# Stage transitions by token tile in a two-block transformer on one core: transposes of the second tile moved among products of the first, and half of the modulations moved to VectorE

## The chip, the cores and the metric

One core of one Trainium2 chip runs the whole program in one launch. The metric is device time in microseconds (us), the median of the timed runs. A lower number is better.

## The reference, cut to what matters

`x` has 256 tokens and 1024 features in fp32. Two blocks follow each other, each of depth 2:

```
# first block; sh, sc, g come from silu(c) @ ada_w + ada_b
h = rms_norm(x, norm_mix[i]) * (1 + sc1) + sh1
y = chunked_relpos_attention(h)  if i == 0 else  chunked_spatial_gating(h)
x = x + g1 * y
h = rms_norm(x, norm_ffn[i]) * (1 + sc2) + sh2
x = x + g2 * (square(relu(h @ w1)) @ w2)          # 1024 -> 4096 -> 1024
# second block
h = rms_norm(x, pre_norm_g[l]);  proj = h @ w_in[l]
y = concat(diff_attention, gqa_attention) @ w_out[l]
x = x + rms_norm(y, post_norm_g[l])
```

So the residual stream `x` goes six times through the same kind of joint: a matmul stage ends, `x` is updated, each token's sum of squares gives a scale, the scaled `x` is transposed and modulated, and the next matmul stage begins. The first joint (the start of the program) and the end are not changed. The five in the middle are called T1 (attention to first mlp), T2 (first mlp to the gate values of spatial gating), T3 (spatial gating to second mlp), T4 (second mlp to the first layer of the second block) and T5 (that layer to the next).

## The kernel before, in words

**Precision.** Every fp32 operand is kept as two parts of type fp32r, a high part and a low part (value minus high part), and a product is three matmuls (`matmul3`, L1596 to L1598): high by high, high by low, low by high.

**Weights.** They stream from memory in chunks of 128 x 2048 through a buffer `raw` of four half chunks (`load`, L357, on the SP queue, which waits until the half four places earlier has been turned into its low part). ScalarE copies a half to `w_hi` (`hi_part`, L534), VectorE subtracts it from raw to get `w_lo` (`lo_part`, L949). `w_hi` and `w_lo` hold four chunks. A chunk is split by both engines in their own written order, and TensorE waits for the low part (`chunk_in`).

**Adaptive rows.** The sums for sh, sc and g (48 + 48 "ada" chunks of 1 MB) are made by VectorE (`ada`, eight instructions at L972 and L976 and a sum at L980), spread over the stages. `columns` (L1663) lets TensorE sum them over partitions, 32 matmuls of one column for a whole set, and `modulation` (three small VectorE instructions) turns them into scale and shift.

**The joint.** VectorE makes the residual (`residual`: product with the gate L1060, sum L1053, per token tile of 128 and half of the columns), ScalarE the sum of squares (`squares`, L551), GpSimd the inverse root (L437, L440), VectorE the scaled tokens `xn` (`norm_x`, L1020). TensorE issues `keep_warm` products with a zero row (L1681, 14 or 16 of them), then `transpose_x`: the 8 transposes of tile 0, then the 8 of tile 1 (L1645), into four banks that each hold both tiles of two feature blocks. ScalarE modulates the pairs of blocks (L560, in the second block L806), VectorE splits them into `h_hi` (L1027) and `h_lo` (L1030) in `operand`. The next stage's first product needs the first pair with both token tiles.

**The mlp stage** (`mlp_stage`) has 8 groups of 512 hidden features: two `up` products with weights as the stationary operand (48 matmuls of 256 columns each, so the result has features on partitions), relu and square on ScalarE (L713, L715) and VectorE (L1278, L1282, `mlp_half`), and two `down` products (24 matmuls of 512 columns each) that accumulate into four banks which were set to zero first (`zero_banks`, L1883). In the first mlp VectorE also makes two ada sums in each group. All engines go through their lists in written order; a wait stops everything behind it on that engine.

## Time and profile before

| | |
|---|---|
| timed runs | 1123.58, 1637.33 and 1128.87 us, median 1128.87 |
| the profiled execution's own time | 1119.04 us |
| its span | 1117.4 us |
| mean granted TensorE clock | 0.957 of full speed |
| TensorE busy (matmuls) | 1073.6 us, 96% |
| VectorE busy | 766.9 us, 69% |
| ScalarE busy | 554.4 us, 50% |

The span runs from the first to the last instruction of one execution. Busy TensorE time counts every matmul, also the products with a zero row, so 96% does not say that 96% of the time goes into products that the result needs. Times in the rows are microseconds from the start of the span.

### The profile page before, as it was taken

What the parts mean: (1) busy time and instruction counts of PE and PEld (TensorE: products, weight loads), DVE (VectorE), ACT (ScalarE), POOL (GpSimd) and SP (SyncE); (2) the same over time, 40 slices, a digit from 0 to 9 for tenths busy, and PEclk for the clock granted to TensorE, in tenths of its full rate; (3) what the DMA queues carried; (4) which work ended last, traced back from release to release, by engine and by line L of the source; (5) the groups of instructions that cost most, each with busy time, mean ns of one, the idle gap of its engine ahead of it and who ended that gap; (6) DMA issues with size and microseconds to landing.
All of it is one profiled execution on the core that took longest, in us unless ns stands there. A gap on an engine that the chain in (4) does not pass through costs nothing.

```text
span 1117.4 us, 18346 instructions
## 1 busy us (share of the span) xinstructions
PE 1073.6 (96%) x6096; PEld 923.0 (83%) x6096; DVE 766.9 (69%) x1352; ACT 554.4 (50%) x933; POOL 94.1 (8%) x146
## 2 busy tenths in 40 slices
PE   6999999999999999999999999999999989799897
PEld 6887776999899788889998789998878768688775
DVE  5798766988876667777877554565487564686573
ACT  1556775354434457444443443454365572556562
POOL 0121101000000100100000000000011020120100
PEclk9799997999999899999999899999999989899999
DMA  9866654778786458765765365456166410457211
GB/s 369 322 242 222 213 191 170 267 279 281 269 297 241 165 191 292 254 231 206 260 224 180 99 214 195 151 190 215 47 220 225 131 57 20 136 200 215 79 33 52
DMA packets 58071, 219.12 MB, mean 196 GB/s; under 512 B 6532, under 2 KB 12420, under 8 KB 51880
## 3 DMA queue, kind: packets, MB, share of 16 engines
q1 hardware_dynamic: 49232, 170.02, 44.5%
q0 software_dynamic: 5760, 41.95, 10.4%
q10 hardware_dynamic: 3032, 6.57, 1.8%
q8 instruction: 24, 0.39, 0.1%
q14 instruction: 23, 0.19, 0.1%
HBM read 217.46 MB, written 1.06 MB: 196 GB/s over the span
## 4 chain that ended last, share of the span: by engine, by line
PE 80%; issue 8%; DVE 4%; DMA 3%; ACT 3%; POOL 1%; DVEq 0%; ACTq 0%; SPq 0%; POOLq 0%
PE ps L1596 24%; PE ps L1597 23%; PE ps L1598 23%; PE ps L1691 2%; DMA ada_raw<-in_adastream 2%; PE ps L1663 2%; PE ps L1681 1%; PE ps L1645 1%; ACT ada_raw L631 1%; DVE w_lo L949 1%; PE ps L1655 1%; POOL rinv L440 1%; PE ps L1958 1%; PE ps L2064 1%; DMA arena<-in_adastream 1%
## 5 line engine op out<-in xcount | busy, mean ns | idle before, releaser
L949 DVE TENSOR_TENSOR w_lo<-raw,w_hi 128x1024 fp32r<-128x1024 f32 (+1 forms) x318 | 358.8, 1171 | 62.0 <-ACT w_hi L534 56.0
L534 ACT ACTIVATE w_hi<-raw 128x1024 fp32r<-128x1024 f32 (+1 forms) x318 | 308.4, 1008 | 129.8 <-DMA raw<-in_wstream 94.2
L1596 PE MATMUL ps<-h_hi,w_hi 128*128 128x256 f32 x704 | 202.3, 287 | 0.5 <-DVE h_lo L1030 0.3
L1597 PE MATMUL ps<-h_lo,w_hi 128*128 128x256 f32 x704 | 200.7, 285 | 0.0
L1598 PE MATMUL ps<-h_hi,w_lo 128*128 128x256 f32 x704 | 200.7, 285 | 0.0
L1596 PE MATMUL ps<-w_hi,h_hi 128*128 128x512 f32 (+1 forms) x480 | 192.7, 401 | 3.2 <-DVE h_lo L1030 3.2
L1597 PE MATMUL ps<-w_lo,h_hi 128*128 128x512 f32 (+1 forms) x480 | 187.3, 390 | 0.0
L1598 PE MATMUL ps<-w_hi,h_lo 128*128 128x512 f32 (+1 forms) x480 | 187.0, 390 | 0.0
L1596 PEld LDWEIGHTS ps<-h_hi,w_hi 128*128 128x128 f32 x704 | 136.6, 194 | 3.5 <-issue 2.0
L1596 PE MATMUL ps<-w_hi,a_hi 128*128 128x512 f32 x352 | 137.4, 390 | 0.7 <-DVE a_lo L1359 0.7
L1597 PEld LDWEIGHTS ps<-h_lo,w_hi 128*128 128x128 f32 x704 | 136.7, 194 | 0.7
L1597 PE MATMUL ps<-w_lo,a_hi 128*128 128x512 f32 x352 | 137.2, 390 | 0.0
L1598 PE MATMUL ps<-w_hi,a_lo 128*128 128x512 f32 x352 | 137.0, 389 | 0.0
L1598 PEld LDWEIGHTS ps<-h_hi,w_lo 128*128 128x128 f32 x704 | 136.5, 194 | 0.0
L1596 PEld LDWEIGHTS ps<-w_hi,h_hi 128*128 128x128 f32 x480 | 92.3, 192 | 24.4 <-DVE h_lo L1030 2.8
L1598 PEld LDWEIGHTS ps<-w_hi,h_lo 128*128 128x128 f32 x480 | 92.4, 193 | 19.0
L1597 PEld LDWEIGHTS ps<-w_lo,h_hi 128*128 128x128 f32 x480 | 92.5, 193 | 16.5
L713 ACT ACTIVATE arena<-ps 128x512 f32<-128x512 f32 x32 | 19.1, 598 | 148.8 <-PE ps L1598 148.8
L1278 DVE TENSOR_TENSOR arena<-arena 128x512 f32<-128x512 f32 x32 | 22.1, 689 | 88.7 <-ACT arena L713 88.7
L1596 PEld LDWEIGHTS ps<-w_hi,a_hi 128*128 128x128 f32 x352 | 66.2, 188 | 14.4 <-issue 1.2
L1598 PEld LDWEIGHTS ps<-w_hi,a_lo 128*128 128x128 f32 x352 | 66.1, 188 | 13.7
L1597 PEld LDWEIGHTS ps<-w_lo,a_hi 128*128 128x128 f32 x352 | 66.2, 188 | 12.9
(186 smaller groups left out, 1341.9 us busy)
## 6 DMA issues: line engine op xcount, KB each, us to landing
raw<-in_wstream SPq DMA_DIRECT2D x296, 512.0 KB, 5.3
ada_raw<-in_adastream POOLq DMA_DIRECT2D x40, 1024.0 KB, 5.1
ada_raw<-in_adastream SPq DMA_DIRECT2D x4, 1024.0 KB, 9.2
arena<-in_adastream SPq DMA_DIRECT2D x4, 1024.0 KB, 10.7
raw<-in_wsmall SPq DMA_DIRECT2D x22, 128.0 KB, 2.2
row<-in_gate_rows ACTq DMA_DIRECT2D x5, 512.0 KB, 4.3
row<-in_params ACTq DMA_DIRECT2D x2, 769.0 KB, 4.1
x<-in_x SPq DMA_DIRECT2D x1, 1024.0 KB, 9.4
```

The source lines that it names most:

```text
L440: nc.gpsimd.tensor_tensor(dst, mean, half[:, 0:cols_n], ALU.pow).then_inc(done, 1)
L534: act.activation(w_hi[:, c % SPLIT, at], raw[:, n, 0:width // 2], ACT.Copy)\
L631: last = act.activation(v, v, ACT.Copy, scale=cond[:, k:k + 1])
L713: act.activation(relu[:, u, :], ps[:, 4 + u, :], ACT.Relu).then_inc(s_upread, 1)
L949: nc.vector.tensor_tensor(w_lo[:, c % SPLIT, at], raw[:, (2 * c + h) % RAW, 0:width // 2], w_hi[:, c % SPLIT, at].bitcast(F32), ALU.subtract)\
L1278: own.inc(nc.vector.tensor_tensor(squared[:, u, :], relu[:, u, :], relu[:, u, :], ALU.mult))
L1596: nc.tensor.matmul(dst, sh, mh, start=start, stop=False)
L1597: nc.tensor.matmul(dst, sh, ml, start=False, stop=False)
L1598: return nc.tensor.matmul(dst, sl, mh, start=False, stop=stop)
L1645: last = nc.tensor.transpose(ps[:, 4 + pr, b * S + t * P:b * S + (t + 1) * P], xn[:, t, k * P:(k + 1) * P], ident[:])
L1663: last = nc.tensor.matmul(ps[:, bank, b:b + 1], ada_acc[:, a, (b % 2) * P:(b % 2 + 1) * P], ones[:, 0:1], start=True, stop=True)
L1691: last = nc.tensor.matmul(ps[:, 0, 2 * a + b:2 * a + b + 1], first_ada[a][:, k, b * P:(b + 1) * P], cond[:, k:k + 1], start=k == 0, stop=k ...
```

## The change

All five joints go tile by tile. (a) The last `down` products of a stage finish token tile 0 before tile 1 begins (`last_downs`), where before only the last of the two hidden parts was ordered by tile; the spatial gating stage now ends so too, with `columns` between the tiles, and without its four closing zero products; in T1 `columns` moves in front of tile 1's last two steps. (b) VectorE's list takes tile 0's residual, tile 1's first half, `norm_x` of tile 0, tile 1's second half, then the operands by tile and by half of the features. (c) TensorE issues 4 zero-row products, transposes tile 0, issues 8 more, and starts products of tile 0; tile 1 is transposed between the first and the second half of those. (d) Features 0 to 3 of each tile (of 8 blocks) are modulated by VectorE, 4 to 7 by ScalarE, in instructions of 128 x 128 instead of 128 x 256. (e) The first group of each mlp is made tile by tile with tokens as the stationary operand. Its result lies with tokens on partitions, so ScalarE copies it out of the bank (`upraw`), TensorE transposes it (`turn_up`, 4 transposes for each half), and only then come relu and square. In this group both `ada` sums stand behind both `mlp_half`, and the second mlp gets two such sums (46 and 47) that the gating stage made before. (f) The second block's joint key and value weights come as one chunk instead of four small ones. (g) The loops over the two halves of the gating stage and over the two layers of the second block are written out.

```diff
-WARM = (14, 16, 16, 16)
+WARM = (4, 8)
...
+            def mlp_first(c0, m0):                              # ScalarE
+                for u in range(2):
+                    act.wait_ge(s_used, c0 + u + 1)
+                    act.activation(squared[:, u, :], ps[:, 2 * u, :], ACT.Copy)\
+                        .then_inc(s_upraw, 1)
+                    act.wait_ge(s_upT, m0 // 14 + u + 1)
+                    act.activation(relu[:, u, :], ps[:, 4 + u, :], ACT.Relu).then_inc(s_upread, 1)
+                    act.wait_ge(s_upread, 2 + m0 + u + 1)
+                    act.activation(a_hi[:, u].rearrange("p a b -> p (a b)"), relu[:, u, :],
+                                   ACT.Square).then_inc(s_acthi, 1)
+                for j in range(4):
+                    split(c0 + 3 + j)
...
+            def operands(n, before_second, behind):             # VectorE
+                operand(0, 0, n)
+                norm_x(1, n)
+                operand(0, 1, n)
+                before_second()
+                operand(1, 0, n)
+                operand(1, 1, n)
+                behind()
+
+            def transition(ready, n, at_first, before_second, behind):
+                residual(0, 0, ready)
+                residual(0, 1, ready)
+                at_first()
+                residual(1, 0, ready)
+                norm_x(0, n)
+                residual(1, 1, ready)
+                operands(n, before_second, behind)
...
+                mlp_half(m0, lambda v: v)                       # first group of an mlp, VectorE
+                split(c0 + 3)
+                mlp_half(m0 + 1, lambda v: v)
+                for a in ((20, 21) if with_ada else (46, 47)):
+                    ada(a)
+                for c in (c0 + 4, c0 + 5, c0 + 6):
+                    split(c)
...
-            keep_warm(7, WARM[0])
-            transpose_x(1)
-            mlp_stage(0, 0, 8, 20, 24)
...
+            def transition(count):                              # TensorE
+                keep_warm(7, WARM[0])
+                transpose_x(0, count)
+                keep_warm(7, WARM[1])
...
+            def last_downs(c, m, between=None):
+                for t in range(TT):
+                    for u in range(2):
+                        if t == 0:
+                            chunk_in(c + 2 + u)
+                            pe.wait_ge(s_act, m + u + 1)
+                        for cb in range(2):
+                            last = down_products(c, u, t, cb, u == 1)
...
+                    if t == 0 and between is not None:
+                        between()
+
+            def mlp_stage(layer, m0, n, a_gate, a_cols):
+                c0 = C_FFN[layer]
+                transition(2 * n)
+                chunk_in(c0)
+                up_tile(c0, 0, 0, range(4), 4 * n + 4)
+                transpose_x(1, 2 * n)
+                up_tile(c0, 0, 0, range(4, KT), 4 * n + 4)
+                chunk_in(c0 + 1)
+                up_tile(c0, 1, 0, range(KT), 4 * n + 4)
+                up_tile(c0, 0, 1, range(KT), 4 * n + 4)
+                up_tile(c0, 1, 1, range(4), 4 * n + 4)
+                turn_up(0, 2 * layer)
+                up_tile(c0, 1, 1, range(4, KT), 4 * n + 4)
+                for bank in (0, 1, 3):
+                    zero_bank(bank)
+                turn_up(1, 2 * layer)
+                zero_bank(2)
+                for u in range(2):
+                    down(c0, u, m0 + u, None, 4, lambda v: v)
+                with pe.Fori(0, 6) as i:
...
-            out_step(2, 0, 1)                                   # T1, TensorE
+            out_step(2, 1, 0)
             pe.wait_ge(s_norm, 16)
             transpose_out(3)
-            out_step(2, 1, 0)
-            out_step(2, 1, 1)
+            out_step(2, 0, 1)
             pe.wait_ge(s_pTc, 16)
             pe.wait_ge(s_ada, 12)
             gate_sum(8, (6, 7))
-            for t in range(TT):
-                for cb in range(2):
-                    out_step(3, cb, t)
+            out_step(3, 0, 0)
+            out_step(3, 1, 0)
+            out_step(2, 1, 1)
             pe.wait_ge(s_ada, 20)
             columns(12, 5)
+            out_step(3, 0, 1)
+            out_step(3, 1, 1)
...
+            project_tile(C_GV, 0, 12, 0, lambda: transpose_x(1, 4))   # T2
+            project_tile(C_GV, 1, 12, 1)
...
+                heads_tile(0)                                   # T4, T5
+                transpose_x(1, layer * 2 + 8)
+                project_tile(CL + 1, 2, layer * 8 + 20, 0)
+                heads_tile(1)
+                project_tile(CL + 1, 3, layer * 8 + 20, 1)
```

The comments behind `#` name engine or place and are not in the code.

## Rows read from the trace of the kernel before

**Rows 1.** Windows: us, busy us and instructions by engine, clock, DMA share, GB/s.

```profile
177.10:193.90 16.80, 15.94 (x67) 9.91 (x66) 10.48 (x20) 6.46 (x13) 3.69 (x5) 0.61 0.45 155
193.90:198.00 4.10, 4.10 (x20) 4.06 (x20) 4.03 (x7) 0.81 (x2) 0.00 (x0) 0.50 0.00 0
382.00:391.30 9.30, 7.44 (x33) 4.48 (x33) 6.84 (x10) 4.01 (x10) 3.17 (x4) 0.70 0.45 159
391.30:396.00 4.70, 4.69 (x11) 3.77 (x12) 2.94 (x6) 2.43 (x5) 0.00 (x0) 0.50 0.18 51
608.10:626.20 18.10, 17.82 (x74) 11.35 (x73) 11.53 (x22) 4.66 (x10) 2.21 (x4) 0.62 0.42 130
808.30:816.60 8.30, 7.22 (x34) 4.18 (x33) 5.93 (x12) 4.61 (x12) 1.95 (x4) 0.79 0.58 186
957.80:970.80 13.00, 7.30 (x34) 4.73 (x33) 8.65 (x17) 7.79 (x17) 3.92 (x7) 0.74 0.49 155
1108.90:1117.40 8.50, 0.12 (x1) 0.00 (x0) 5.36 (x10) 1.30 (x4) 1.56 (x3) 0.73 0.30 123
```

**Rows 2.** Timeline around T2: start, us, engine, line, operation, idle before it.

```profile
382.05 3.62 PE L1681 MATMUL ps<-zero_row 1*128 1x512 bf16 x16
...
388.23 1.97 PE L1645 MATMUL ps<-ident,arena 128*128 128x128 f32 x8 [0.75 <-DVE arena L1020]
...
391.31 0.77 PE L1596 MATMUL ps<-w_hi,h_hi 128*128 128x512 f32 x1 [1.11 <-DVE h_lo L1030]
```

**Rows 3.** Timeline of ScalarE in the second mlp: relu of both halves.

```profile
655.60 0.60 ACT L713 ACTIVATE arena<-ps 128x512 f32<-128x512 f32 x1 [8.07 <-PE ps L1598]
661.36 0.60 ACT L713 ACTIVATE arena<-ps 128x512 f32<-128x512 f32 x1 [0.71 <-PE ps L1598]
678.02 0.60 ACT L713 ACTIVATE arena<-ps 128x512 f32<-128x512 f32 x1 [8.60 <-PE ps L1598]
```

**Rows 4.** Timeline of VectorE in the first mlp: one ada sum and splits.

```profile
210.32 0.35 DVE L972 TENSOR_SCALAR ada_acc<-ada_raw,cond 128x256 f32 x1
...
213.69 4.62 DVE L949 TENSOR_TENSOR w_lo<-raw,w_hi 128x1024 fp32r<-128x1024 f32 x4
218.23 0.35 DVE L972 TENSOR_SCALAR ada_acc<-ada_raw,cond 128x256 f32 x1
```

**Rows 5.** Groups of instructions, shapes apart: count, busy us, mean ns, idle before.

```profile
L1030 DVE TENSOR_TENSOR h_lo<-arena,h_hi 128x512 fp32r<-128x512 f32 x24 | 16.6, 692 | 0.8
L1020 DVE TENSOR_SCALAR arena<-x,rinv 128x1024 f32<-128x1024 f32 x12 | 9.0, 752 | 8.3 <-POOL rinv L440 6.6 <-issue 1.4
L1512 DVE TENSOR_SCALAR arena<-ps,recip 128x128 f32<-128x128 f32 x16 | 4.8, 342 | 0.0
L440 POOL TENSOR_TENSOR rinv<-mean,half 128x1 f32<-128x1 f32 x16 | 11.6, 727 | 1.3
L551 ACT ACTIVATE arena<-x 128x1024 f32<-128x1024 f32 x12 | 12.7, 1056 | 30.3 <-DVE x L1053 20.0 <-DMA x<-in_x 8.7 <-DVE x L1585 1.5
```

**Rows 6.** Page, DMA issues: KB each, us to landing.

```profile
raw<-in_wstream SPq DMA_DIRECT2D x296, 512.0 KB, 5.3
```

**Rows 7.** Timeline: `columns` in the first mlp's end, T1, T3; last scaled ada of T1.

```profile
170.19 3.31 ACT L631 ACTIVATE ada_raw<-ada_raw,cond 128x256 f32<-128x256 f32 x8 [2.28 <-DMA ada_raw<-in_adastream]
178.09 4.42 PE L1663 MATMUL ps<-ones,ada_acc 128*128 128x1 f32 x32 [0.86 <-DVE ada_acc L1199]
360.24 3.63 PE L1663 MATMUL ps<-ones,ada_acc 128*128 128x1 f32 x32
609.19 5.34 PE L1663 MATMUL ps<-ones,ada_acc 128*128 128x1 f32 x32
```

**Rows 8.** Timeline of TensorE in T5: the transposes.

```profile
966.07 3.58 PE L1645 MATMUL ps<-ident,arena 128*128 128x128 f32 x16 [4.59 <-DVE arena L1020]
```

**Rows 9.** Windows inside T5: columns as in the first group.

```profile
968.50:969.00 0.50, 0.50 (x4) 0.50 (x3) 0.00 (x0) 0.50 (x2) 0.00 (x0) 0.50 0.74 180
969.50:970.00 0.50, 0.15 (x2) 0.00 (x0) 0.43 (x1) 0.50 (x3) 0.00 (x0) 1.00 0.99 410
```

More of the change, by code:

```diff
@@ L60 @@
 C_SECOND = C_FFN[1] + 32
-C_LAYER = 20
+C_LAYER = 17
 assert C_GU + 24 == C_FFN[1]
@@ L487, in _ @@
             norm(3)
-            with pool.Fori(0, DEPTH) as layer, own.loop(layer, DEPTH, 15):
+            for layer in range(DEPTH):
                 for t in range(TT):
@@ new lines, in _, with lsplit @@
+            square(0, 5)
+            load_row(gate_rows[3:4, :].to_broadcast([P, D]))
+            square(1, 6)
+            modulate(0, 3, mod_scale[:, 3], mod_shift[:, 3])
+            modulate(1, 3, mod_scale[:, 3], mod_shift[:, 3])
+            split(C_FFN[1] + 2)
+            mlp_stage(1)
+            for layer in range(DEPTH):
+                CL = C_SECOND + layer * C_LAYER
+                def lsplit(k):
+                    split(CL + k)
+                act.wait_ge(s_h, layer * 8 + 16)
+                act.dma_start(prenorm[:], prenorm_in[layer]).then_inc(s_pre, 16)
+                square(0, layer * 2 + 7)
+                square(1, layer * 2 + 8)
@@ L1092, in _ @@
             first_sum(0)
-            norm_x(0)
+            for t in range(TT):
+                norm_x(t, 0)
             first_sum(2)
@@ L1636, in project, with project_tile @@
+            def project_tile(c, bank, h_base, t, between=None):
+                for half in range(2):
+                    chunk_in(c + half)
+                    for n in range(4):
+                        k = half * 4 + n
+                        operand_in(h_base, t, k)
+                        last = matmul3(ps[:, bank, :], tokens(k, t), weights(c + half, 512, n),
+                                       k == 0, k == KT - 1)
                     if t == 1:
                         last.then_inc(s_used, 1)
-            def transpose_x(n, turn4=0, turn2=0):
+                    elif half == 1:
+                        last.then_inc(s_half, 1)
+                    if half == 0 and between is not None:
+                        between()
@@ L1896, in up, with up_tile, turn_up @@
                 last.then_inc(s_used, 1)
-            def down(c, u, m, i, per, turn, ends=False):
+            def up_tile(c, u, t, ks, h_base):
+                for k in ks:
+                    operand_in(h_base, t, k)
+                    last = matmul3(ps[:, 2 * u, t * AW:(t + 1) * AW], tokens(k, t),
+                                   weights(c + u, AW, k), k == 0, k == KT - 1)
+                if t == 1 and ks[-1] == KT - 1:
+                    last.then_inc(s_used, 1)
+            def turn_up(u, count):
+                pe.wait_ge(s_upraw, count + u + 1)
+                for b in range(2):
+                    for t in range(TT):
+                        last = nc.tensor.transpose(
+                            ps[:, 4 + u, b * S + t * P:b * S + (t + 1) * P],
+                            squared[:, u, t * AW + b * P:t * AW + (b + 1) * P], ident[:])
+                last.then_inc(s_upT, 1)
@@ new lines, in zero_bank, with down_products @@
+            def zero_bank(bank):
+                nc.tensor.matmul(ps[:, bank, :], zero_row[:], zeros4, start=True, stop=False)
+            def down_products(c, u, t, cb, ends=False):
+                for b in range(2):
+                    v = slice(t * P, (t + 1) * P)
+                    wh, wl = weights(c + 2 + u, D, b)
+                    n = slice(cb * 512, (cb + 1) * 512)
+                    last = matmul3(ps[:, cb * 2 + t, :], (a_hi[:, u, b, v], a_lo[:, u, b, v]),
+                                   (wh[:, n], wl[:, n]), False, ends and b == 1)
+                return last
@@ L1899, in down @@
+            def down(c, u, m, i, per, turn):
                 chunk_in(c + 2 + u, i, per)
                 pe.wait_ge(s_act, turn(m + 1))
-                for t, cb in ((0, 0), (0, 1), (1, 0), (1, 1)):
-                    bank = cb * 2 + t
-                    for b in range(2):
-                        v = slice(t * P, (t + 1) * P)
-                        wh, wl = weights(c + 2 + u, D, b)
-                        n = slice(cb * 512, (cb + 1) * 512)
-                        last = matmul3(ps[:, bank, :], (a_hi[:, u, b, v], a_lo[:, u, b, v]),
-                                       (wh[:, n], wl[:, n]), False, ends and b == 1)
-                    if ends and (t, cb) != (1, 1):
-                        last.then_inc(s_bank, 1)
```

643 lines of the change are left out of this document (338 added, 305 removed).

## The prediction

> **What bounds the kernel now.** I read the windows of the granted clock and busy time first, then the timeline at each joint, then the groups for durations. In the mlp, gating and projection stages TensorE issues products without a gap, and the waits inside the attentions are not touched, so the change acts on what the joints cost and on whatever new wait it makes between products. The windows between the last product of a stage and the first of the next are 16.8 (T1), 9.3 (T2), 18.1 (T3), 8.3 (T4) and 13.0 us (T5), and 8.5 us behind the last product of all [rows 1]. The reader is to see that TensorE is "busy" for 15.9 of the 16.8 and 17.8 of the 18.1 us: it makes zero-row products, transposes and `columns`, none of it product. Two stages then begin at the half clock (1.2 instead of 2.4 GHz, clock 0.50), 4.1 us long behind T1 and 4.7 us behind T2 [rows 1]; half of that time is lost, 2.0 and 2.3 us. So the joints cost 18.8, 11.6, 18.8 (with 0.7 us of small waits for operands), 8.3 and 13.0 us: 70.5 in all. Only this can be won. The chain inside is seen at T2: behind the zero-row products tile 1's transposes wait 0.75 us for `norm_x`, and the first product 1.11 us for `h_lo` [rows 2]. Both are waits for one chain of VectorE, ScalarE and GpSimd that starts only with the last product.
>
> **Unit prices.** The relus of the two halves are 5.76 us apart, for 48 matmuls of 256 columns: 0.12 each; a group takes 22.42 us, so 48 matmuls of 512 columns take 22.42 - 11.52 = 10.9, 0.227 each [rows 3]. A zero-row product takes 3.62/16 = 0.226, a transpose 1.97/8, some 0.23 without the tail [rows 2]. On VectorE an ada sum takes 213.69 - 210.32 = 3.37, a chunk's low part 2.3 (4.54 for four halves) [rows 4], `norm_x` 0.75, the operand's subtraction 0.69 (the cast of the same shape less), ScalarE's square sum 1.06, GpSimd's power 0.73 [rows 5].
>
> **The new joint at full clock.** Let E be the end of a stage's last product. Tile 1's first bank is done at E-1.36 (6 matmuls); VectorE makes product and sum (1.3) and `norm_x` of tile 0 (0.75): E+0.9, hidden behind four zero-row products (0.9). Transposes of tile 0: E+1.0 to 2.9. Eight zero-row products: to E+4.7. VectorE in that time modulates four 128 x 128 blocks. No such row exists; the nearest, a scaled copy out of PSUM of that size, is 0.34 [rows 5], the other end is 0.27 where two overlap. With cast and subtraction, at most 0.69 each, the operand is ready between E+4.4 and 4.8, so products begin at E+4.7. Tile 1's eight transposes come on top later, 1.8. The joint costs 6.5 us, bound by TensorE's own list. Tile 0's second half stands on VectorE behind `norm_x` of tile 1, so it needs tile 1's residual (E+2.1), square sum, GpSimd, that `norm_x` and its own split: E+6.8, covered where its first half's products take 2.7 us (T2), and 0.7 late where they take 1.4 and no transposes stand between (T4).
>
> **T2**: 6.5 against 11.6. Half-speed products may come back; bounds 0 and 2.3 by the same rows, I take 1.2, since 8 zero-row products and two sets of transposes are little work for the clock: 7.7, gain 3.9 (2.8 to 5.1). **T4**: 6.5 + 0.7, and 1.1 for the clock: 8.3 against 8.3, gain 0 (-1.2 to 1.1). **T5**: the output is normed before the residual, so `norm_x` of tile 0 stands behind tile 1's sums of squares and its inverse root and products. ScalarE squares the last bank (E+1.0), GpSimd needs three steps (E+2.3), VectorE multiplies both halves (1.4) and then makes `norm_x` (0.75): E+4.5. Four transposes, then VectorE's sums of tile 1 and its operand (3.4 together): first product at E+8.2; with the transposes of tile 1 and small waits 10.5, and 0.5 for the clock: 11.0 against 13.0, gain 2.0 (0 to 2.5). The single key and value chunk and the four halves at the very end that go away save VectorE and ScalarE time beside TensorE's: 0. The last 8.5 us are the chain of tile 1 and stay. Of the queues: ScalarE's row load sits between its two squares as before and costs its list 0.3 us inside a wait; SP's raw loads for chunks 3 and 4 follow the low parts of chunks 1 and 2, which now come behind E, and land 5.3 us later [rows 6], before ScalarE asks for them at E+22. Both are priced at nothing; without that cover the loads would add to the wait for chunk 4 below.
>
> **T3.** Now comes what eats the gain. `columns` lies between the tiles, but it is still in TensorE's list: 3.6 us at full clock and 5.3 where the clock falls in it [rows 7], taken 4.4. The earlier need of the second half's `a_lo` costs 0.4. Tile 1's 24 products follow `columns` and may be at half speed: 0 to 2.3, taken 1.2. Joint 6.5. Turning the first group costs 8 more transposes (1.8), its zero products 0.9, and 0.3 until ScalarE's copy of the second bank. So the first `down` begins at E+4.7+11.5+1.8+1.8+0.9+0.3 = E+21. **VectorE's order** then matters. Its split of chunk 3 stands before `mlp_half` of the second half, and ScalarE's high part of chunk 3 stands behind its own work on that half, which ends at E+22.3. So VectorE, idle since E+19.8, gets chunk 3 at E+25.6, the half at E+27.0; TensorE waited 0.6 and ends `down` at E+32.5. VectorE has two ada sums (6.7) in front of chunk 4, which TensorE needs now: E+36.0, a wait of 3.5. Before, no ada sum was here. Sum: 4.4+0.4+1.2+6.5+1.8+0.9+0.3+4.1 = 19.6, with 0.5 for a clock that falls behind E: 20.1 against 18.8: a loss of 1.3 (gain 3 to loss 5).
>
> **T1.** The last scaled ada chunk leaves ScalarE at 173.5 [rows 7]; `columns` started 4.6 us later. Of these a half chunk's high and low part took some 2.2, one on each engine [rows 4], and the low part now stands behind. So `columns` can start at 176.0 (ada sum 19 is in the tree form, 2.4 us). Its place in TensorE's list is reached two steps of six matmuls (1.4 each) before the old end of 177.1: 174.3. That is 1.8 us of waiting, where it was 0.9. `columns` 4.4 as before. The two steps behind it at half speed: 0 to 2.7, taken 2.2. Joint 6.5, turning and zeros 3.0 as in T3. The same debt of 4.1 on VectorE, and here it goes on: chunk 6's raw halves can load only behind chunk 4's low part and land 5.3 later [rows 6], then another ada sum comes before `mlp_half`; I get waits of 1.4 and 0.5 in the second group, none from the third, since VectorE needs 18.8 us for a group (2 x 3.37 + 4 x 2.3 + 4 steps of 0.7, the shape of the subtraction) of TensorE's 22.4. Sum: 1.8+4.4+2.2+6.5+3.0+4.1+1.9 = 23.9 against 18.8: loss 5.1 (2 to 8).
>
> **Clock and transposes.** In T5 TensorE had been idle for 4.6 us, then made only the 16 transposes from 966.1 to 969.6, and the clock went from 0.50 to 1.00 before any product [rows 8, 9]. The Trainium skill says the contrary (TensorE: Matmul & The Clock Gate, Part 4: PE-mode transpose): transposes do not count as busy for the clock in the way that matmuls do. This rule speaks against a change that puts them among products. The trace does not agree, and the sum stays with the trace; by the rule the clock would fall in each joint, which the next part prices from rows.
>
> **Sum.** -3.9 + 0 - 2.0 + 1.3 + 5.1 = +0.5 us on the profiled 1119.04: 1119.5. The timed median of 1128.87 is pulled up by one run of 1637; the two others have their middle at 1126.2, 7 us above the profiled one. I predict 1126.2 + 0.5, some 1127 us: no change. A measurement of this kernel can tell about 2%, 22 us, from nothing.
>
> **Rivals.** *The joints' gain arrives (0.20).* The clock stays full and VectorE's debt hides, because ScalarE or the raw loads are earlier than I count. T1 18.8 - 16.7, T2 5.1, T3 18.8 - 13.6, T4 1.1, T5 2.5: 16 us less, 1110. For it: 14 or 16 zero-row products in each joint become 12, and no engine has more work. Against it: the written order of ScalarE. *The clock (0.15, the page's rule belongs here).* It falls in every joint: T2, T4, T5 at their upper bounds (1.1, 1.2 and 2.0 more), T1 at 0.5 more behind `columns` and 1.1 behind E, T3 at 1.1 and 1.0: 8 more, 1135. For it: it fell in all five joints [rows 1]. *VectorE's debt is not paid back in the first mlp (0.07), the slow side.* Each group has 22.4 - 18.8 = 3.6 us to spare; if the raw landing behind a late split takes over 3.6 us longer than 5.3, each of the seven groups left starts late by the rest. At 5.8 longer that is 2.2 x 7 = 15, and with the clock's 8: +23 over the forecast, 1150, slower. It decides from a landing of 8.9 us. For it: two ada loads of 1 MB share the DMA engines with each group. Against it: before, the same loads left no wait. *It does not do what it says (0.08)*: tile 0's products do not begin before tile 1 is done, because a weight chunk or `norm_x` of tile 1 is late; T2, T4 and T5 stay as they were and turning is paid twice: +12, 1139.
>
> **Chances.** My forecast, within 5 us of 1127, has 0.50. The range 1106 to 1142 takes in the first two rivals and most of the last, with 5 us for runs that differ as 1123.58 and 1128.87 do. Faster by over 2% needs 22 us, more than the first rival gives: 0.07. Slower by over 2%: 0.06, from the debt that stays. Within 2%: 0.87.
>
> **What the new profile would show.** First product 4.7 us behind the last one in T2, T3 and T4, about 8 in T5. Waits of TensorE for `w_lo` of some 3.5 us, once in each mlp, behind the first group's `down`; VectorE idle for 5 and 3 us before. `columns` starting near 176 and three gaps there. Clock 0.50 over some of the products behind `columns`. The forecast is wrong if no wait for `w_lo` stands in the first groups, or if the clock is full through all joints.

## Result and the profile after

The changed kernel takes 1134.13 us (median of 12 runs, 1126.40 to 1138.92), the kernel before 1122.64 (12 runs, 1115.81 to 1637.33). The ratio is 1.0088 with a 95% interval of 1.0055 to 1.0121: 0.9% slower, 9.9 us of 1122.6. It is made from fast runs alone, without the one of 1637.33, so it is not the quotient of the two medians, which differ by 11.5 us. The forecast was a difference of +0.5 us.

The two profiled executions have spans of 1117.4 and 1133.2 us, 15.8 apart. To see where, I cut both at rows that stand in both traces: the gate sums of the first mlp's start and end, the last mix of the gating, the gate sums of the second mlp, the key transposes of either layer, and the first filler of T5. A filler is one of the zero-row products in a joint. The first fence has the windows of the kernel before, the second those of the changed one, T1 to T5 in order (us, busy us and instructions by engine, clock, DMA share, GB/s). Each holds its joint and what follows up to the next cut.

```profile
169.88:352.77 182.89, 182.03 (x1108) 161.32 (x1107) 150.68 (x243) 87.72 (x109) 11.68 (x20) 0.95 0.74 260
352.77:589.69 236.92, 234.35 (x1365) 206.20 (x1364) 170.61 (x255) 114.68 (x152) 16.64 (x24) 0.97 0.66 228
589.69:784.17 194.48, 194.01 (x1194) 171.64 (x1193) 113.96 (x137) 87.85 (x106) 2.21 (x4) 0.96 0.52 175
784.17:855.39 71.22, 70.14 (x380) 59.04 (x379) 48.28 (x85) 33.95 (x54) 8.47 (x13) 0.98 0.47 154
957.85:1009.56 51.71, 46.01 (x228) 37.72 (x228) 39.83 (x72) 28.73 (x45) 10.73 (x16) 0.93 0.58 195
```

```profile
172.42:364.39 191.97, 186.68 (x1120) 166.08 (x1118) 155.25 (x253) 88.19 (x111) 10.35 (x20) 0.95 0.71 250
364.39:597.00 232.61, 231.04 (x1361) 203.81 (x1360) 170.75 (x263) 113.99 (x152) 17.23 (x24) 0.99 0.67 233
597.00:794.18 197.18, 192.86 (x1194) 172.55 (x1193) 117.18 (x145) 88.16 (x108) 1.55 (x4) 0.97 0.52 172
794.18:865.84 71.66, 69.60 (x376) 58.75 (x375) 51.16 (x87) 32.72 (x48) 8.48 (x13) 0.98 0.49 165
968.22:1021.87 53.65, 48.56 (x223) 38.77 (x223) 39.15 (x73) 23.63 (x39) 10.11 (x16) 0.90 0.48 160
```

The reader is to see length minus busy of TensorE, its idle time, and the clock. Summed over windows of 1 us, busy time times (1 minus clock) is what the half clock costs. What is left is work at full clock:

```
stage        before: length idle clock work    after: length idle clock work    change
T1           182.9   0.9   8.5  173.5           192.0   5.3  10.2  176.5        +9.1
T2           236.9   2.6   5.9  228.4           232.6   1.6   3.4  227.6        -4.3
T3           194.5   0.5   6.8  187.2           197.2   4.3   6.5  186.4        +2.7
T4            71.2   1.1   1.5   68.6            71.7   2.0   1.6   68.1        +0.4
T5            51.7   5.7   1.6   44.4            53.7   5.1   5.0   43.6        +1.9
sum          737.2  10.8  24.3  702.1           747.1  18.3  26.7  702.1        +9.9
```

The stages that the change touches are 9.9 us longer, which is also what the timed runs say; the work is the same, idle time has 7.5 us more and the clock 2.4. The other 5.9 us of the spans lie in the attentions: 17 us at half clock in the first one where there were 3.4, and a clock loss of 6.3 instead of 1.7 us in the last. Across the kernels below that loss is anything from 0 to 6.6, with the same code, so it belongs to the execution.

The joints themselves, windows of the changed kernel (T1's first products, T2 twice, T4 twice, T5 twice: joint, then first products):

```profile
195.60:201.40 5.80, 5.80 (x27) 5.80 (x28) 5.70 (x11) 1.17 (x4) 0.00 (x0) 0.50 0.29 88
393.60:398.40 4.80, 3.97 (x21) 1.82 (x20) 4.70 (x11) 2.53 (x7) 0.79 (x2) 1.00 0.02 9
398.40:402.20 3.80, 3.75 (x11) 3.04 (x12) 2.73 (x4) 0.96 (x2) 0.00 (x0) 0.64 0.00 0
818.50:823.10 4.60, 3.96 (x22) 1.85 (x21) 4.34 (x10) 2.34 (x6) 1.03 (x2) 0.96 0.30 95
823.10:826.20 3.10, 3.10 (x14) 3.10 (x15) 2.78 (x4) 1.15 (x2) 0.25 (x1) 0.51 0.33 121
968.20:978.40 10.20, 6.50 (x22) 2.89 (x21) 8.64 (x16) 5.21 (x11) 3.65 (x7) 0.73 0.53 182
978.40:983.90 5.50, 5.50 (x30) 5.50 (x30) 1.41 (x2) 0.00 (x0) 0.00 (x0) 0.57 0.30 95
```

T2's joint is 4.8 us where it was 9.3, T4's 4.6 where it was 8.3, T5's 10.2 where it was 13.0 [rows 1]. Behind each, products run at half clock: all of the 5.8 us in T1, most of the 3.8, 3.1 and 5.5 in T2, T4 and T5. The timeline of TensorE in T2 answers to [rows 2]:

```profile
393.69 1.03 PE L1789 MATMUL ps<-zero_row 1*128 1x512 bf16 x4
394.65 1.09 PE L1748 MATMUL ps<-ident,arena 128*128 128x128 f32 x8
395.67 1.90 PE L1789 MATMUL ps<-zero_row 1*128 1x512 bf16 x8
398.45 0.47 PE L1676 MATMUL ps<-w_hi,h_hi 128*128 128x512 f32 x1 [0.88 <-DVE h_lo L1073]
```

Eight transposes take 1.09 us at full clock, and the next row begins 1.02 us behind their start; the 1.97 of [rows 2] was a row at half clock. TensorE's own list ends at 397.6, and the first product waits 0.88 us for the operand. VectorE has the longer list here:

```profile
395.14 0.69 DVE L1105 TENSOR_TENSOR x<-x,arena 128x512 f32<-128x512 f32 x1
395.75 1.36 DVE L1060 TENSOR_SCALAR arena<-ps,mod_scale,mod_shift 128x128 f32<-128x128 f32 x4
```

It begins the four modulations of tile 0 only behind tile 1's residual (L1105), when all eight transposes have ended, so faster transposes of tile 0 would not make this joint shorter. TensorE's waits (us in total, times, longest us):

```profile
PE ps L1676 <- DVE w_lo L979: 9.4, 4, 3.3
PE ps L1748 <- DVE arena L1047: 3.7, 1, 3.7
PE ps L1676 <- DVE h_lo L1073: 2.3, 4, 0.9
PE ps L1771 <- DVE ada_acc L1243: 1.5, 1, 1.5
```

Four waits for `w_lo`: 3.30 us behind the first group of the first mlp, 3.29 in the second, 1.42 and 1.39 in T4 and T5. The timeline of the three engines around the first:

```profile
210.57 0.69 DVE L1342 TENSOR_TENSOR arena<-arena 128x512 f32<-128x512 f32 x1 [5.30 <-ACT arena L723]
213.88 3.89 ACT L529 ACTIVATE w_hi<-raw 128x1024 fp32r<-128x1024 f32 x4
214.96 2.36 DVE L979 TENSOR_TENSOR w_lo<-raw,w_hi 128x1024 fp32r<-128x1024 f32 x2 [2.96 <-ACT w_hi L529]
218.57 0.34 DVE L1002 TENSOR_SCALAR ada_acc<-ada_raw,cond 128x256 f32<-128x256 f32 x1
...
224.94 0.43 DVE L1010 TENSOR_TENSOR ada_acc<-ada_acc,ada_odd 128x256 f32<-128x256 f32 x1
225.28 4.63 DVE L979 TENSOR_TENSOR w_lo<-raw,w_hi 128x1024 fp32r<-128x1024 f32 x4
227.78 0.38 PE L1676 MATMUL ps<-h_hi,w_hi 128*128 128x256 f32 x1 [3.30 <-DVE w_lo L979]
```

VectorE is idle for 5.30 and 2.96 us, gets chunk 3's high part only behind ScalarE's work on both halves (ScalarE's four high parts begin at 213.88), then makes two ada sums (218.57 to 225.3) in front of chunk 4's low parts, for which TensorE waits 3.30 us. About 1 us behind the end of that wait the clock falls to 0.50 for 3.4 us (228.8 to 232.2), and the same happens in the second mlp.

### The profile page after: what moved, and what is told of

It is laid out like the page before. It is cut to its first block, busy times and chain, and to the rows that moved or that the text cites. A ratio compares the mean times of both kernels' runs of the same rounds, so it can differ in the third digit from the quotient of the medians.

```text
span 1133.2 us, 17002 instructions
## 1 busy us (share of the span) xinstructions
PE 1084.4 (96%) x6090; PEld 934.4 (82%) x6090; DVE 775.7 (68%) x1374; ACT 547.8 (48%) x918; POOL 91.0 (8%) x146
## 3 DMA queue, kind: packets, MB, share of 16 engines
q0 software_dynamic: 5760, 41.95, 10.2%
## 4 chain that ended last, share of the span: by engine, by line
PE 85%; DVE 8%; DMA 3%; ACT 2%; issue 1%; POOL 0%; SPq 0%; DVEq 0%; POOLq 0%; ACTq 0%
PE ps L1676 25%; PE ps L1677 24%; PE ps L1678 24%; DVE w_lo L979 2%; PE ps L2238 2%; PE ps L1799 2%; PE ps L1771 2%; PE ps L2276 1%; PE ps L1763 1%; DMA ada_raw<-in_adastream 1%; DMA raw<-in_wstream 1%; ACT ada_raw L639 1%; PE ps L1789 1%; PE ps L2123 1%; PE ps L1748 1%
## 5 line engine op out<-in xcount | busy, mean ns | idle before, releaser
L979 DVE TENSOR_TENSOR w_lo<-raw,w_hi 128x1024 fp32r<-128x1024 f32 x300 | 356.2, 1227 | 60.8 <-ACT w_hi L529 55.3
L529 ACT ACTIVATE w_hi<-raw 128x1024 fp32r<-128x1024 f32 x300 | 305.0, 1054 | 133.4 <-DMA raw<-in_wstream 105.8
L1676 PE MATMUL ps<-w_hi,h_hi 128*128 128x512 f32 (+1 forms) x544 | 216.1, 397 | 5.2 <-DVE w_lo L979 2.8
L1677 PE MATMUL ps<-w_lo,h_hi 128*128 128x512 f32 (+1 forms) x544 | 209.0, 384 | 0.0
L1678 PE MATMUL ps<-w_hi,h_lo 128*128 128x512 f32 (+1 forms) x544 | 208.8, 384 | 0.0
L1676 PE MATMUL ps<-h_hi,w_hi 128*128 128x256 f32 x640 | 184.3, 288 | 6.6 <-DVE w_lo L979 6.6
L1677 PE MATMUL ps<-h_lo,w_hi 128*128 128x256 f32 x640 | 183.2, 286 | 0.0
L1678 PE MATMUL ps<-h_hi,w_lo 128*128 128x256 f32 x640 | 183.2, 286 | 0.0
L1676 PEld LDWEIGHTS ps<-w_hi,h_hi 128*128 128x128 f32 x544 | 108.1, 199 | 30.2 <-issue 6.8
L1677 PEld LDWEIGHTS ps<-w_lo,h_hi 128*128 128x128 f32 x544 | 108.4, 199 | 16.4
L735 ACT ACTIVATE arena<-ps 128x512 f32<-128x512 f32 x28 | 16.7, 596 | 111.7 <-PE ps L1678 111.7
```

The lines of the kernel that those rows point to most:

```text
L529: act.activation(w_hi[:, c % SPLIT, at], raw[:, n, 0:width // 2], ACT.Copy)\
L735: act.activation(relu[:, u, :], ps[:, 4 + u, :], ACT.Relu).then_inc(s_upread, 1)
L979: nc.vector.tensor_tensor(w_lo[:, c % SPLIT, at], raw[:, (2 * c + h) % RAW, 0:width // 2], w_hi[:, c % SPLIT, at].bitcast(F32), ALU.subtract)\
L1676: nc.tensor.matmul(dst, sh, mh, start=start, stop=False)
L1677: nc.tensor.matmul(dst, sh, ml, start=False, stop=False)
L1678: return nc.tensor.matmul(dst, sl, mh, start=False, stop=stop)
```

## Experiments

Each kernel is the changed one (1.0088) with the edit shown, unless said otherwise; the ratio is to the kernel before. "Stage" is the length as in the table above. Stage lengths are from one profiled execution and the clock in them can differ by some 5 us in T1 and T3, so I read idle and clock apart. Some of these executions lie far from their kernel's median: e1's was 7.8 us slower, e5's 9.8, e12's 8.0 and e13's 3.8 us faster. Where sums of stages and timed runs disagree, the timed runs decide.

**e1: ada sums behind the chunk.**

```
                 mlp_half(m0 + 1, lambda v: v)
+                split(c0 + 4)
                 for a in ((20, 21) if with_ada else (46, 47)):
                     ada(a)
-                for c in (c0 + 4, c0 + 5, c0 + 6):
+                for c in (c0 + 5, c0 + 6):
```

> The changed kernel with one edit on VectorE: in the first group of both mlps the low parts of the second group's first chunk come ahead of the two ada sums, not behind them. Theory A (VectorE's written order is the debt): the chunk's low part is ready at about 221 instead of 227.6 us, so both waits of TensorE for w_lo (3.30 and 3.29 us) go, and with them the two stretches at half clock behind them (3.4 us each, 1.7 lost): 10 us less, 1124 us, ratio to the kernel before about 1.001. Rival B (the debt only moves: the ada sums now stand in front of the second chunk's low part, needed 5.8 us later): the waits come back one chunk later, 0 to 3 us saved, 1131 to 1134 us.

1123.79 us, ratio 1.0023 (0.9997 to 1.0048). Both waits of 3.3 us for `w_lo` and the two stretches behind them are gone: in T1 and T3 together idle 9.6 to 6.4, clock 16.7 to 13.3, lengths 188.5 and 194.6. Of the 10 us expected, 6.1 show in the stages and some 7 in the timed runs, for other waits came (two rows of TensorE, then two of ScalarE):

```profile
237.46 0.47 PE L1677 MATMUL ps<-w_hi,a_hi 128*128 128x512 f32 x1 [1.05 <-DVE a_lo L1346]
...
670.76 0.47 PE L1677 MATMUL ps<-w_hi,a_hi 128*128 128x512 f32 x1 [2.05 <-DVE a_lo L1346]
...
661.96 1.06 ACT L529 ACTIVATE w_hi<-raw 128x1024 fp32r<-128x1024 f32 x1 [3.21 <-DMA raw<-in_wstream]
664.39 1.06 ACT L529 ACTIVATE w_hi<-raw 128x1024 fp32r<-128x1024 f32 x1 [1.38 <-DMA raw<-in_wstream]
```

In T1 the second group's own ada sum stands ahead of `mlp_half`. T3 has none there: its two ada sums still stand ahead of the low parts of chunks 5 and 6 (654.7 to 659.3), the raw halves that load behind these come late to ScalarE (3.21 and 1.38 us), and VectorE's `mlp_half` stands behind the split that waits for them. So the order is a cause, and part of the debt moved, in T3 by way of the loads.

**e5: order mended on both engines.**

```
 ScalarE: +  split(c0 + 3)            (ahead of mlp_first, not behind it)
 VectorE:    split(c0 + 3); ada(first); mlp_half(m0); mlp_half(m0 + 1)
             split(c0 + 4); ada(second); split(c0 + 5); split(c0 + 6)
```

> The changed kernel with the written order of the first group mended on both engines in both mlps: ScalarE and VectorE split chunk 3 ahead of the first half's work, VectorE makes one ada sum ahead of it, then both halves, then chunk 4, then the other ada sum. Theory A (the order is the debt, the moved ada sum of the second group only showed a rest of it): no wait for w_lo or a_lo over 0.5 us in the first two groups, T1 (from its gate sums to those at the end of the first mlp) 187.4 us where the changed kernel had 192.0 and the last experiment 188.5, T3 192.3 where they had 197.2 and 194.6: 9.5 us under the changed kernel, 1124 us. Rival B (the raw loads bound the first two groups, not the order): waits come back at other places, T1 188.5, T3 194.6, as in the experiment before.

1118.49 us, ratio 0.9958 (0.9918 to 0.9998): 15 us under the changed kernel, and just faster than the kernel before. No wait for `w_lo` is left in T1 and T3, and the longest for `a_lo` is 0.48 us; idle is 3.5 us in both stages together instead of 9.6. T1 is 182.5 and T3 191.7. In T1 some 5 us more than the order explains are the clock: `columns` ran mostly at full clock in this execution. Rival B, that the raw loads bound it whatever the order, fell.

**e2: both halves of the second value chunk early (T4, T5).**

```
                 modulate(0, layer + 4, prenorm, None)
                 hi_part(CL + 2, 0, CW)
+                hi_part(CL + 2, 1, CW)
                 modulate(1, layer + 4, prenorm, None)
-                hi_part(CL + 2, 1, CW)
```

and VectorE's `split` of that chunk ahead of tile 1's operand.

> The changed kernel with one edit at T4 and T5: ScalarE's high part and VectorE's low part of the second half of the second value chunk come ahead of the modulation of tile 1 instead of behind it. Theory A: both engines are idle there for 1.7 us and more, so TensorE's two waits for w_lo (1.42 and 1.39 us) go and nothing comes in their place: 2.8 us less, 1131 us. Rival B: the low part (2.3 us for both halves, VectorE was idle 1.7) delays tile 1's operand by 0.6 us and TensorE waits for h_lo there: 1.6 us less or nothing.

1123.69 us, ratio 1.0025 (0.9999 to 1.0052). Both waits are gone, T4 69.9 instead of 71.7 and T5 51.0 instead of 53.7, in all 4.4: the 2.8 expected and some clock. The timed gain, 7 us, is larger; the interval of either ratio is 6 to 7 us wide, and T1 to T3 are within 0.3 us of the changed kernel's, so the rest stays unexplained.

**e3: no second fillers.** `WARM = (4, 0)`.

> The changed kernel without the eight zero-row products between tile 0's transposes and its first product, in all five joints. Theory A (they are cover only, the clock falls whatever they do): TensorE waits about 1.5 us for the operand instead, first product 0 to 0.3 us earlier in T1 to T4; in T5, where they ran at half clock in 3.6 us and stood in front of a ready operand, 2 us earlier: 2 to 3 us less, 1131 us. Rival B (they hold the clock, and transposes do not): half-clock stretches of 3.4 us or more grow behind each joint, 1.7 us or more lost in each of four: 5 us or more on top, 1139 us.

1125.49 us, ratio 1.0044 (1.0022 to 1.0066). T1 is 1.4, T3 1.0 and T5 2.4 us shorter, T2 0.3 longer, T4 the same. The clock loss went from 26.7 to 20.6: rival B is wrong, eight fillers of one zero row do not hold the clock. In T5 they stood in front of a ready operand: without them the first product comes 8.2 us behind the last one of the stage before, with them 10.2.

**e4: 20 fillers in T5 instead of 4.** `keep_warm(7, 20 if layer else 4)` ahead of tile 0's transposes. (The kernel before had 16 there, not 20.)

> The changed kernel with 20 instead of 4 zero-row products ahead of tile 0's transposes in T5 alone (as many as the kernel before had between its last product and its wait). They fill the 3.7 us in which TensorE waits for norm_x. Theory A (the idle time is what drops the clock in T5): the stretch at half clock, 11 us long from 973 to 984, gets shorter by 7 us or goes, the second zero-row products take 1.8 instead of 3.6 us, and the transition is 3 to 5 us shorter: 1130 us. Rival B: zero-row products do not count for the clock; it falls as before and T5 stays at 53.7 us from its first row to the key transposes: no change, 1134 us.

1131.06 us, ratio 1.0088 (1.0056 to 1.0119); T5 53.6 us as before. Timeline and windows:

```profile
966.36 4.49 PE L1789 MATMUL ps<-zero_row 1*128 1x512 bf16 x20
971.09 1.97 PE L1748 MATMUL ps<-ident,arena 128*128 128x128 f32 x8 [0.24 <-DVE arena L1047]
972.99 3.59 PE L1789 MATMUL ps<-zero_row 1*128 1x512 bf16 x8
```

```profile
966.00:976.60 10.60, 10.36 (x39) 4.45 (x38) 9.04 (x16) 5.21 (x11) 3.64 (x7) 0.73 0.48 175
976.60:981.80 5.20, 5.20 (x27) 5.20 (x28) 1.35 (x2) 0.00 (x0) 0.00 (x0) 0.56 0.29 101
```

TensorE is busy for 10.36 of 10.60 us, and still its clock is 0.50 by the transposes (1.97 us for eight) and behind them. So it is not the idle time alone that drops it. Theory A fell; the question became what the fillers are.

**e9 and e10: fillers that use 128 rows.**

```
-    nc.tensor.matmul(ps[:, bank, :], zero_row[:], zeros4, start=True, stop=True)
+    nc.tensor.matmul(ps[:, bank, :], block_row[:],
+                     block_row[:].unsqueeze(1).to_broadcast([P, 4, P]),
+                     start=True, stop=True)
```

`block_row` is 128 x 128 bf16, ones in e9 and zeros in e10. This also changes the fillers at the kernel's start.

> The changed kernel with other fillers in the joints: the 4 and 8 products of one zero row become products of a 128 x 128 block of ones with 512 columns, into the same bank, as many and as long. Theory A (the clock falls because the fillers use one row of the array and change nothing in it): the half-clock stretches behind the joints of T2, T4 and T5 go, of the 26.7 us that the clock costs in the five joints some 10 are won, 1124 us. Rival B (the clock falls from what lies before the fillers, the waits and the one-column products of columns, and what the fillers are does not matter): stretches and stage times as in the changed kernel within 1 us, 1134 us.

> As the run before, with a block of zeros instead of ones. Theory A1 (rows in use are what matters): as with ones. Theory A2 (the data that toggle matter): as in the changed kernel, 1134 us. Rival B (neither matters): both runs as in the changed kernel.

e9: 1117.06 us, ratio 0.9958 (0.9929 to 0.9986). e10: 1115.55 us, 0.9952 (0.9922 to 0.9983). Clock loss in the five stages 26.7 to 16.3 and 16.1, idle time up by 1.7. The windows of e9 in T2, joint and first products:

```profile
390.10:394.90 4.80, 3.79 (x21) 1.91 (x20) 4.70 (x11) 2.52 (x7) 0.79 (x2) 1.00 0.02 8
394.90:399.60 4.70, 4.65 (x24) 3.94 (x25) 3.90 (x8) 1.69 (x5) 0.00 (x0) 1.00 0.17 46
```

They are at clock 1.00, where the changed kernel had 0.64 behind the joint. A filler takes as long as before (eight in 1.89 us). Ones or zeros make no difference; one row or 128 does. Both operands went from one row to 128 together, so which of them matters is open. Of the 14.6 us that e9 gains in the timed runs, 8.7 show in the five stages.

**e11: the kernel before with fillers of ones.**

> The kernel before with its fillers (14, 16, 14 to 18 and 17 zero-row products) as products of a full block of ones. Theory A: of the 24.3 us that the clock costs in its five joints 8 or more are won, ratio 0.993 or less. Rival B: no change, ratio 1.000.

1109.66 us, ratio 0.9902 (0.9867 to 0.9936); clock loss 24.3 to 13.9 (T1 3.4, T2 4.2, T3 3.4, T4 1.5 less, T5 2.1 more), idle time 4.7 more, since fillers at full clock end earlier. So this gain has nothing to do with the change. In the five stages 5.4 of its 11 us show; where the rest comes from is not shown.

**e13 against e4: T5 again.** e13 is the changed kernel with e5's order, e2's halves, fillers of ones and 20 of them in T5.

> The kernel of the last run with 20 instead of 4 fillers of ones ahead of tile 0's transposes in T5. With one zero row as filler these 20 changed nothing (T5 53.6 us, clock loss 5.1 us in both). Theory A (rows of the array in use are what holds the clock): the stretch at half clock in T5, 8 us long, goes, T5 47.0 us where the last run had 49.8, 1104 us. Rival B (in T5 the attention's last part or the idle time ahead of it drops the clock whatever fills the wait): T5 49.8 us, 1107 us.

```profile
941.76 4.49 PE L1792 MATMUL ps<-block_row 128*128 128x512 bf16 x20
946.58 1.09 PE L1751 MATMUL ps<-ident,arena 128*128 128x128 f32 x8 [0.33 <-DVE arena L1050]
947.51 1.89 PE L1792 MATMUL ps<-block_row 128*128 128x512 bf16 x8
950.10 0.36 PE L1679 MATMUL ps<-w_hi,h_hi 128*128 128x256 f32 x1 [0.70 <-DVE h_lo L1076]
```

```profile
941.70:950.10 8.40, 7.38 (x38) 3.52 (x37) 7.17 (x13) 4.07 (x10) 3.29 (x7) 1.00 0.56 176
950.10:954.00 3.90, 3.39 (x26) 3.19 (x27) 3.57 (x5) 2.10 (x3) 0.26 (x1) 1.00 0.26 97
```

The clock is 1.00 throughout, with the same count of fillers as in e4. It takes both: in e9, e10 and e12, where 4 fillers of 128 rows left TensorE idle for 3.8 us, the clock fell in T5 too and cost 2.7 to 3.0 us. T5 is 48.7 us, 1.0 under its predecessor and not the 2.8 expected: the operand of VectorE now comes last (0.70 us). The time, 1107.43 us (ratio 0.9886, 0.9847 to 0.9925), is that of the predecessor.

**e6 and e14: the first groups not turned.** PE makes tile 1's transposes right behind the second fillers, then `zero_banks()` and `up` for both halves; ScalarE and VectorE in the order of the other groups. e6 has nothing else, e14 is e13 with this.

> The changed kernel with the first group of both mlps made as before: its up products put features on partitions and start when both tiles' operands are there, no copy and no transposes of the product, ScalarE and VectorE in the order of the other groups. Joints stay tile by tile up to there. Theory A (turning with its debt costs more than the early start gives): T1 185, T3 190 us instead of 192.0 and 197.2, in all 14 us less, 1120 us. Rival B (the early start is worth what it was meant to be): the joints get 4 to 6 us longer, which eats turning's 2 us and most of the debt: 4 us less or nothing, 1130 to 1134 us.

> As the run before, with the first group of both mlps made as in the kernel before (features on partitions, nothing turned). Theory A (with the order mended and the clock held, the early start pays for the turning and no more): T1 and T3 each within 2 us of the run before (185.9 and 188.1 us in its predecessor), the medians within 3 us. Rival B (turning still costs): T1 and T3 3 us shorter each, 6 us faster than the run before. Rival C (turning pays): 3 us longer each.

e6: 1125.46 us, ratio 1.0033 (1.0006 to 1.0060), T1 188.1 and T3 192.5: 8.6 us less in the two stages and 6 in the timed runs, between theory A (14) and rival B (4 or nothing). e14: 1112.24 us, ratio 0.9913 (0.9882 to 0.9943), T1 187.7 and T3 194.4, where e13 has 185.0 and 189.7. TensorE's timeline in e6 shows what an untiled start costs, waits for tile 1's `norm_x` and for its operand (here T1):

```profile
196.54 1.97 PE L1750 MATMUL ps<-ident,arena 128*128 128x128 f32 x8 [1.05 <-DVE arena L1047]
...
202.43 0.55 PE L1678 MATMUL ps<-h_hi,w_hi 128*128 128x256 f32 x1 [2.11 <-DVE h_lo L1073]
```

In e14 the second of them is 3.83 us in T1, and the clock losses are 6.8 and 6.3 us against 5.0 and 1.7. So turning cost time mainly through the order written around it. Whether it pays with that mended is not shown: the two stages are 7.3 us longer without it (rival C), but 6.4 of these are the clock of single executions, and the timed ratios differ by 0.0027, inside their intervals.

**e8: ScalarE makes all modulations.** VectorE's four are moved to ScalarE, one signal for each half.

> The changed kernel with one part undone: ScalarE makes all eight modulations of a tile, VectorE none. Theory A (VectorE's half is needed to have the operand ready when the second zero-row products end): the first half's operand is ready 0.4 us later, behind ScalarE's square of tile 1 it may be 1 us, and the second half's 1.5 us later; 0.5 to 2 us in each of the five joints, 5 us more in all, 1139 us. Rival B (it is hidden either way): the joints stay within 0.3 us, 1134 us.

1135.22 us, ratio 1.0113 (1.0068 to 1.0158). The stages are 11.6 us longer, half of it clock (26.7 to 33.0) and half idle time (18.3 to 24.1), most of it in T2, T4 and T5; the timed ratios differ by 0.0025, inside their intervals. The first product waits where it waited 0.88 and 0.64 us (T2, T4):

```profile
398.23 0.77 PE L1661 MATMUL ps<-w_hi,h_hi 128*128 128x512 f32 x1 [2.10 <-DVE h_lo L1058]
...
825.28 0.55 PE L1661 MATMUL ps<-w_hi,h_hi 128*128 128x256 f32 x1 [1.73 <-DVE h_lo L1058]
```

VectorE's half is not what cost time; the waits for the operand grow without it.

**e7 and e12: what paid, together.** e7 has e5's order, e2's halves and no second fillers in T1, T3 and T5. e12 has e5's order, e2's halves and all fillers of ones.

> The changed kernel with all edits that paid: the mended order of the first groups, both halves of the second value chunk ahead of tile 1's modulation in T4 and T5, and no second zero-row products in T1, T3 and T5. If the savings add up: T1 186, T2 232.6, T3 191.4, T4 69.9, T5 48.7 us, 18 us under the changed kernel and 8 us under the kernel before: 1114 us, ratio 0.993. Rival (the clock takes it back: with fewer fillers the half-clock stretches grow): 1120 us or more.

> The changed kernel with the mended order of the first groups, both halves of the second value chunk early, the second fillers kept, and all fillers as products of a full block of ones. If the order saves what it saved alone (T1 and T3 some 9 us together) and fillers of ones hold the clock (theory A): 1107 us, ratio 0.985. If the kind of filler does not matter (rival B): 1116 us, ratio 0.994, and the version without second fillers in T1, T3 and T5 (1112.8 us) stays the best.

e7: 1112.76 us, ratio 0.9914 (0.9886 to 0.9943), as expected; its T2 was 2.4 us longer than forecast, 3.1 of clock more and 0.4 of idle less. e12: 1107.18 us, ratio 0.9883 (0.9844 to 0.9922). Against e11, the kernel before with the same fillers (0.9902), the change with its order mended is 8 us better in the profiled stages (723.9 against 731.8), 4.3 of them clock, and 2 us in the timed runs, within their intervals. So with the same fillers no gain of the change is shown. e12's T3 has no clock loss at all. In T1 of e12 and e13 a wait of 1.9 us for `a_lo` is left in the first group (0.48 in e5), and VectorE works without a pause ahead of it, an ada sum of 3.4 us included: the mended order has too little room once TensorE comes sooner.

```
kernel                           T1     T2     T3    T4    T5   idle  clock   ratio
before                         182.9  236.9  194.5  71.2  51.7  10.8  24.3   1
changed                        192.0  232.6  197.2  71.7  53.7  18.3  26.7   1.0088
e5 order                       182.5  230.8  191.7  71.0  53.1  12.4  14.5   0.9958
e9 fillers of ones             188.4  231.0  196.2  71.1  51.7  20.0  16.3   0.9958
e11 before, fillers of ones    181.6  234.3  191.4  71.0  53.5  15.5  13.9   0.9902
e12 order, halves, fillers     185.9  230.8  188.1  69.3  49.8  12.9   9.6   0.9883
```

## Why the prediction was right and wrong

The forecast of no change held by the 2% it named, and 1134 lies in its range, though not within 5 us of 1127; but the kernel is measurably slower, by 9.9 where 0.5 was forecast. The waits came where they were forecast. One term was far too small and another too large, and that they partly cancelled is luck.

- **T2** was forecast to gain 3.9 and gained 4.3; the first product came 4.8 us behind the last one, forecast 4.7. The place is right and its reason is not: the forecast had TensorE's own list as the bound, with the operand ready at E+4.4 to 4.8; the list ended at E+3.9, and the operand was the bound. **T4**: 0 forecast, 0.4 lost, with a first product at 4.6, and a wait of 1.42 for `w_lo` that the forecast does not have.
- **VectorE's order** was right to the row: the wait for chunk 4 forecast at 3.5 us measured 3.30 and 3.29, VectorE's idle times forecast at 5 and 3 us measured 5.30 and 2.96. e1 and e5 show it as the cause. The further waits of 1.4 and 0.5 in T1's second group did not come (0.2 us at most).
- **The failed step is the price of the clock.** Place by place, from windows of 0.5 us of the changed kernel (us lost):

```
                                              forecast  measured
T1  `columns` and the two steps behind it        3.0       5.1
T1  behind the joint                             0         3.3
T1  behind the wait for `w_lo`                   0         1.7
T2  behind the joint                             1.2       1.7
T3  `columns` and the products behind it         2.0       1.7
T3  end of the joint and behind it               0.5       3.1
T3  behind the wait for `w_lo`                   0         1.7
T4  behind the joint                             1.1       1.5
T5  from the transposes of tile 0 on             0.5       5.1
sum                                              8.3      24.9
```

  The table of stages has 26.7: another 1.7 lies in T2 ahead of the joint, in the kernel before as well, and was no part of the forecast. The places that the forecast left out or nearly so are the products behind T1's and T3's joints, those behind both waits for `w_lo`, and T5, where its own eight fillers ran at half clock. e2 and e4, whose edits don't touch T1 to T3, lose 10.2, 3.4 and 6.6 or 6.7 us there, as the changed kernel does (10.2, 3.4, 6.5), so this is not one odd execution. The rows for it were there: the products behind T1 and T2 ran at half clock, and the clock was 0.61 and 0.62 over the joints of T1 and T3 [rows 1].
- **Unit price of a transpose**: 0.23 us was read from a row at half clock [rows 2]; at full clock it is 1.02/8 = 0.13. The forty of tile 1 and the sixteen that turn stand in TensorE's way, 56 in all, some 6 us too much. The forty of tile 0 cost less than forecast too, but in T2, T3 and T4 the first product then waited 0.88, 0.60 and 0.64 us for VectorE's operand. With the 1.9 us of waits forecast in T1's second group, of which at most 0.2 came, this hid almost half of the miss in the clock. With the right price of a transpose alone the forecast would have been a gain of some 5 us.
- **T5** was forecast to gain 2.0 and lost 1.9. `norm_x` came at E+4.7 as forecast (E+4.5), but then eight transposes and eight fillers ran at half clock (rows below), so the first product came at E+10.2 and not E+8.2; then the first products ran at half clock and `w_lo` was 1.39 us late. The 8.2 was right for the operand, as e3 shows, though its terms, added one behind the other (4.5, four transposes, 3.4), give 8.8; what it left out is the fillers at half clock in front of it.

```profile
968.22 1.03 PE L1789 MATMUL ps<-zero_row 1*128 1x512 bf16 x4
972.96 1.97 PE L1748 MATMUL ps<-ident,arena 128*128 128x128 f32 x8 [3.70 <-DVE arena L1047]
974.86 3.59 PE L1789 MATMUL ps<-zero_row 1*128 1x512 bf16 x8
```

- **T1** was forecast to lose 5.1 and lost 9.1, **T3** 1.3 and lost 2.7: in both the wait for chunk 4 came as forecast, the clock cost 7.1 and 4.0 us more than its terms, and the cheaper transposes, in T1 also the waits that did not come, gave part of that back.
- **Rivals.** The clock rival had the time (1135) and in part the place: the clock fell in all five joints, though T2 lost less by it than before (3.4 us instead of 5.9). The rule put beside it does not hold here. In e9 to e12 only the fillers changed, all transposes stayed, and in e12 T3 has 24 transposes, 16 of them between products, and no clock loss. The Trainium skill (TensorE: Matmul & The Clock Gate, Part 4: PE-mode transpose) has transposes not counting as busy in the way that matmuls do. The traces here show no fall that comes with them once the fillers have 128 rows (e12's T3, 0.0 us lost). The debt that stays, the joints' gain and the change that does nothing did not happen.

## What to carry to other kernels

Read unit prices from rows whose clock you know, and price the half clock as a term of its own, from windows: stretch by stretch, with those that a new wait would add. When a transition is cut finer, the written order on the other engines has to be cut with it: the idle time of VectorE ahead of a late operand is the sign, and a sum that nobody waits for yet belongs into that gap. A filler meant to hold TensorE's clock should use all 128 rows: it costs the same time as one of a single row. Before a gain is read from one profiled execution, see how far its own time lies from the kernel's median.

## What was not expected of the hardware

- Products of one zero row (1 x 128 by 512 columns) did not hold the clock, although TensorE was busy for 10.36 of 10.60 us with them, transposes and a last few products; as many of 128 rows, ones, held it at 1.00 (e13). It is not a matter of one execution: in T2's joint or right behind it the clock fell in all ten kernels with fillers of one row and in none of the six with 128 rows (ones or zeros), in T4's in eight of the ten (not in e5 and e7) and in none of the six. Which other counts of rows would do wasn't tried.
- The fillers alone were worth more than the change: 1.3% (1.0088 to 0.9958) and 1.0% (1 to 0.9902), not all of which shows in the five stages.
- In untouched attention stages the clock loss of single executions went from 0 to 6.6 us. Why is open.
